# Two model blocks on one core: memory products placed between the features behind each norm, one modulation chunk's columns moved behind a gathering, and half of two norms' squares moved to VectorE

## The reference, cut to what matters

```python
for layer in range(DEPTH):                                  # first block
    mod = (c_act @ ada_w[layer] + ada_b[layer])[:, None, :]
    sh1, sc1, g1, sh2, sc2, g2 = jnp.split(mod, 6, axis=-1)
    h = rms_norm(x, norm1_g[layer]) * (1.0 + sc1) + sh1
    x = x + g1 * mixer(h)                                   # even or odd mixer
    h = rms_norm(x, norm2_g[layer]) * (1.0 + sc2) + sh2
    x = x + g2 * grouped_moe(h, ...)
for layer in range(DEPTH):                                  # second block
    x = x + rms_norm_2(mixer_2(rms_norm_2(x, g[0])), g[1])
    mem_n = rms_norm_2(mem, mem_norm_g[layer])
    k = mem_n @ wk[layer]; v = mem_n @ wv[layer]            # 256 x 256 each: the "memory products"
    q = rms_norm_2(x, g[2]) @ wq[layer]
    x = x + rms_norm_2(softmax_attention(q, k, v) @ wo[layer], g[3])
    x = x + rms_norm_2(swiglu(rms_norm_2(x, g[4]), ...), g[5])
```

## Time and profile before

| | before |
|---|---|
| median of 3 runs | 1759.46 us (1755.81 to 1762.49) |
| the profiled execution, its own time | 1757.93 us |
| its span in the trace | 1756.1 us |
| PE busy | 1672.5 us (95%) |
| DVE busy | 1272.7 us (72%) |
| ACT busy | 1091.1 us (62%) |
| HBM read | 411.21 MB, 235 GB/s over the span |
| mean granted PE clock | 0.983 of 2.4 GHz |

### The profile page before, as it was taken

How to read it: one execution, slowest core, us unless ns; L and a number is a source line. 1 busy time by engine, 2 the same in 40 slices (tenths; PEclk the granted TensorE clock), 3 DMA queues, 4 the chain that set the end, 5 groups by cost and what they waited for, 6 DMA issues and landing times.

```text
span 1756.1 us, 25101 instructions
## 1 busy us (share of the span) xinstructions
PE 1672.5 (95%) x8563; PEld 1355.7 (77%) x8563; DVE 1272.7 (72%) x2053; ACT 1091.1 (62%) x1681; POOL 13.1 (1%) x27
## 2 busy tenths in 40 slices
PE   5998999999999999999999898899999998999998
PEld 3875778888878767888888786678888776878886
DVE  3874598988977586989989656666666656676665
ACT  3545488888864464887988655665444547564443
POOL 1000000000000000000000000000000000000000
PEclk8999899999999998999999999999999999999999
DMA  9878489999977573999999654115565561325552
GB/s 367 301 266 330 183 323 331 383 330 348 370 260 262 192 222 114 354 325 376 340 334 384 233 168 144 49 72 193 182 200 187 163 215 49 136 91 183 191 191 72
DMA packets 113346, 413.37 MB, mean 235 GB/s; under 512 B 13024, under 2 KB 13072, under 8 KB 112880
## 3 DMA queue, kind: packets, MB, share of 16 engines
q1 hardware_dynamic: 110208, 400.74, 64.3%
q0 software_dynamic: 1936, 8.59, 1.5%
q10 hardware_dynamic: 1120, 2.99, 0.4%
HBM read 411.21 MB, written 1.05 MB: 235 GB/s over the span
## 4 chain that ended last, share of the span: by engine, by line
PE 78%; DVE 8%; ACT 7%; issue 3%; DMA 3%; DVEq 0%; ACTq 0%; SPq 0%
PE banks L794 17%; PE banks L796 16%; PE banks L795 16%; PE banks L1604 9%; PE banks L1605 5%; DVE weights_low L2309 2%; PE banks L966 2%; ACT weights_high L2016 1%; DMA weight_ring<-in_exp_w_gate 1%; PE banks L925 1%; PE banks L824 1%; DMA weight_ring<-in_ada_w 1%; ACT qk_features L1925 1%; PE banks L851 1%; ACT scratch L1863 1%
## 5 line engine op out<-in xcount | busy, mean ns | idle before, releaser
L2309 DVE TENSOR_TENSOR weights_low<-weight_ring,weights_high 128x1024 fp32r<-128x1024 f32 (+1 forms) x656 | 769.3, 1218 | 145.1 <-ACT weights_high L1691 84.7
L794 PE MATMUL banks<-weights_high,features_parts 128*128 128x512 f32 (+1 forms) x1488 | 591.8, 398 | 11.8 <-DVE features_parts L2573 3.6
L796 PE MATMUL banks<-weights_high,features_parts 128*128 128x512 f32 (+1 forms) x1488 | 580.9, 390 | 0.0
L795 PE MATMUL banks<-weights_low,features_parts 128*128 128x512 f32 (+1 forms) x1488 | 580.4, 390 | 0.0
L2016 ACT ACTIVATE weights_high<-weight_ring 128x1024 fp32r<-128x1024 f32 x384 | 392.9, 1061 | 80.6 <-PE banks L796 52.9
L794 PEld LDWEIGHTS banks<-weights_high,features_parts 128*128 128x128 f32 x1488 | 280.9, 189 | 78.6 <-issue 13.3
L796 PEld LDWEIGHTS banks<-weights_high,features_parts 128*128 128x128 f32 x1488 | 280.5, 189 | 59.9
L795 PEld LDWEIGHTS banks<-weights_low,features_parts 128*128 128x128 f32 x1488 | 281.1, 189 | 55.3 <-issue 0.7
L1691 ACT ACTIVATE weights_high<-weight_ring 128x1024 fp32r<-128x1024 f32 (+1 forms) x176 | 176.9, 1044 | 125.6 <-PE banks L796 45.0
L1604 PE MATMUL banks<-features_parts,weights_high 128*128 128x512 f32 x704 | 250.7, 400 | 1.1 <-DVE features_parts L2448 1.0
L1605 PE MATMUL banks<-features_parts,weights_low 128*128 128x256 f32 x704 | 197.7, 281 | 0.0
(11 more groups left out here) (413 smaller groups left out, 1626.1 us busy)
## 6 DMA issues: line engine op xcount, KB each, us to landing
weight_ring<-in_exp_w_gate SPq DMA_DIRECT2D x128, 512.0 KB, 5.2
weight_ring<-in_exp_w_up SPq DMA_DIRECT2D x128, 512.0 KB, 5.1
weight_ring<-in_exp_w_down SPq DMA_DIRECT2D x128, 512.0 KB, 5.3
weight_ring<-in_ada_w SPq DMA_DIRECT2D x84, 512.0 KB, 5.5
weight_ring<-in_ffn_wg SPq DMA_DIRECT2D x44, 512.0 KB, 4.1
weight_ring<-in_ffn_wu SPq DMA_DIRECT2D x44, 512.0 KB, 4.5
weight_ring<-in_ffn_wd SPq DMA_DIRECT2D x44, 512.0 KB, 4.1
weight_ring<-in_even_w_in SPq DMA_DIRECT2D x28, 512.0 KB, 5.7
```

What stands on the lines that cost most here:

```text
L794: eng.matmul(dst, lh, rh, start=first, stop=False, **kw)
L795: eng.matmul(dst, lh, rl, start=False, stop=False, **kw)
L796: mm = eng.matmul(dst, ll, rh, start=False, stop=last, **kw)
L2309: V(half_of(low(s), i, size), half_of(slot(n), i, size), half_of(high(s), i, size).bitcast(F32), ALU.subtract)\
```

## The change

It does five things, named as above.

(a) In `experts(0)` the four products of `modulate(15)` go behind `gather(0)`, and the two filling products go out.
(b) Behind the first experts PE makes 12 memory steps, and the last 4 stand one by one ahead of the turns 4 to 7, where the 8 filling products were.
(c) In the two norms ACT squares row block 0 alone, and DVE squares row block 1 with one `tensor_tensor_reduce`.
(d) In `cross(l)` PE makes 8 steps, waits until DVE has copied the last output chunk of the mixer (bank 5 or 7, where the second half of the product now goes), makes 2 steps, and puts the last 6 one by one ahead of the products k = 2 to 7. ACT copies the two halves with two instructions.
(e) In `feed_forward(0)` it makes 10 steps, and the last 6 likewise ahead of k = 2 to 7.

In the diff `norm_x(n)` and `take_mem_apart` are ACT's functions, `square_second_rows` is DVE's, and the others are PE's; ACT's `norm_whole_x` changes as `norm_x(n)` does.

```diff
-                    if i >= 4 and busy:
-                        stay_busy(4, busy[i - 4])
+                    ahead(i)
...
-            def by_feature(source, first=0):
+            def by_feature(source, first=0, between=lambda k: None):
                 def fresh(k):
                     if 1 <= k < 5:
                         turn_feature(source, k + 3, first=first)
+                    between(k)
                     features_wait()
...
-                if step == 2 * KD - 1:
-                    mm.then_inc(mem_used, 1)
+                    if step == 2 * KD - 1:
+                        mm.then_inc(mem_used, 1)
...
+                stay_busy(0, 0 if l == 0 else 4)
+                eng.wait_ge(rows_by_vector, 6 * l + 2)
+                gather(5 * l)
                 if l == 0:
                     modulate(15, 6, at=260)
-                stay_busy(0, 2 if l == 0 else 4)
-                eng.wait_ge(rows_by_vector, 6 * l + 2)
-                gather(5 * l)
...
-            mem_steps(16, [half_of(B[5], i, 512) for i in range(2)])
-            turn_normed("a1h1", (2, 2, 2, 2))
+            first_memory = [half_of(B[5], i, 512) for i in range(2)]
+            mem_steps(12, first_memory)
+            turn_normed("a1h1", lambda i: mem_steps(1, first_memory) if i >= 4 else None)
...
-                mem_steps(16, [B[2 + i][:, S:2 * S] for i in range(2)])
-                fresh = features_of_x(busy=0)
+                memory = [B[2][:, S:2 * S], B[5 + 2 * l][:, 0:S]]
+                mem_steps(8, memory)
+                eng.wait_ge(copied["dve"], chunks[st[("ev_out", "od_out")[l]][1][1][1]]["done"])
+                mem_steps(2, memory)
+                fresh = features_of_x(busy=0, between=lambda k: mem_steps(1, memory) if k >= 2 else None)
...
+                memory = [B[2 + i][:, S:2 * S] for i in range(2)]
                 if l == 0:
-                    mem_steps(16, [B[2 + i][:, S:2 * S] for i in range(2)])
-                fresh_x = features_of_x(4, 12 * l)
+                    mem_steps(10, memory)
+                fresh_x = features_of_x(4, 12 * l, lambda k: mem_steps(1, memory) if l == 0 and k >= 2 else None)
...
             def norm_x(n):
                 warm(ACT.Sqrt)
+                eng.wait_ge(x_ready, 2 * n - 1)
+                square(NB[:, 0, :], X[:, 0, :], 0)
+                eng.wait_ge(squares, sq[0])
...
+            def take_mem_apart(m, halves):
+
+                kind, l = MEM_ORDER[m]
+                eng.wait_ge(mem_used, m + 1)
+                for i in range(2):
+                    ins = eng.activation((MK if kind == "k" else MV)[l][:, i, :], halves[i], ACT.Copy)
+                ins.then_inc(mem_taken, 1)
...
+            def square_second_rows(at):          # DVE
+
+                eng.tensor_tensor_reduce(NB[:, 1, :], X[:, 1, :], X[:, 1, :], 1.0, 0.0, ALU.mult, ALU.add, SS[:, at:at + 1])\
+                   .then_inc(var_ready, 1)
```

More of the change, by code:

```diff
@@ L812, in stay_busy, with turn @@
                                start=True, stop=True, skip_group_check=True)
-            def turn(name, source, busy=()):
+            def turn(name, source, ahead=lambda i: None):
                 first, items = turns[name]
@@ L872, in by_pair, with features_of_x @@
                     features_wait()
-            def features_of_x(first=0, busy=12):
+            def features_of_x(first=0, busy=12, between=lambda k: None):
                 for tb in range(TB):
@@ L881, in features_of_x @@
                         turn_feature(of_x, k, [tb], first)
-                return by_feature(of_x, first)
+                return by_feature(of_x, first, between)
             def chunk(q, steps, fresh=None):
@@ L966, in mem_steps, with turn_normed @@
                     mm = eng.matmul(halves[i], left, right, start=k == 0, stop=k == KD - 1)
-                if step == 2 * KD - 1:
-                    mm.then_inc(mem_used, 1)
+                    if step == 2 * KD - 1:
+                        mm.then_inc(mem_used, 1)
             normed_n = [0]
-            def turn_normed(name, busy=()):
+            def turn_normed(name, ahead=lambda i: None):
                 normed_n[0] += 1
                 eng.wait_ge(normed, normed_n[0])
-                turn(name, lambda i, tb: NB[:, tb, i * 128:(i + 1) * 128], busy)
+                turn(name, lambda i, tb: NB[:, tb, i * 128:(i + 1) * 128], ahead)
             def attention(pairs, between=lambda t: None, first=lambda t: None):
@@ L1771, in norm_x @@
                 warm(ACT.Sqrt)
+                eng.wait_ge(x_ready, 2 * n - 1)
+                square(NB[:, 0, :], X[:, 0, :], 0)
+                eng.wait_ge(squares, sq[0])
                 for tb in range(TB):
-                    if n:
-                        eng.wait_ge(x_ready, 2 * n - 1 + tb)
-                    elif tb == 0:
-                        eng.wait_ge(x_loaded, 16)
-                    square(NB[:, tb, :], X[:, tb, :], tb)
-                    if n:
-                        eng.wait_ge(squares, sq[0])
-                        eng.activation(ROOT[:, tb:tb + 1], SS[:, tb:tb + 1], ACT.Sqrt, scale=1.0 / D, bias=EPS_[:, :])\
-                           .then_inc(root_ready, 1)
-                if not n:
-                    eng.wait_ge(squares, sq[0])
-                    take_root(SS, TB, D)
+                    if tb:
+                        roots[0] += 1
+                        eng.wait_ge(var_ready, roots[0])
+                    eng.activation(ROOT[:, tb:tb + 1], SS[:, tb:tb + 1], ACT.Sqrt, scale=1.0 / D, bias=EPS_[:, :])\
+                       .then_inc(root_ready, 1)
             def norm_and_take_raw(l):
@@ L1829, in norm_whole_x @@
                 warm(ACT.Sqrt)
+                eng.wait_ge(x_ready, done - 1)
+                square(NB[:, 0, :], X[:, 0, :], 4)
+                eng.wait_ge(squares, sq[0])
                 for tb in range(TB):
-                    eng.wait_ge(x_ready, done - 1 + tb)
-                    square(NB[:, tb, :], X[:, tb, :], 4 + tb)
-                    eng.wait_ge(squares, sq[0])
+                    if tb:
+                        roots[0] += 1
+                        eng.wait_ge(var_ready, roots[0])
                     eng.activation(ROOT[:, 2 + tb:3 + tb], SS[:, 4 + tb:5 + tb], ACT.Sqrt, scale=1.0 / D, bias=EPS_[:, :])\
@@ L2201, in cross @@
                 eng.wait_ge(features_split, features[0] + 8)
-                take_mem(1 + 2 * l, PS[:, 2:4, S:2 * S])
+                take_mem_apart(1 + 2 * l, (B[2][:, S:2 * S], B[5 + 2 * l][:, 0:S]))
                 take_chunks(st[f"caq{l}"][1], lambda i: QK[:, i, :])
@@ L2362, in normalise @@
                 ins.then_inc(normed, 1)
+            def square_second_rows(at):
+                eng.tensor_tensor_reduce(NB[:, 1, :], X[:, 1, :], X[:, 1, :], 1.0, 0.0, ALU.mult, ALU.add, SS[:, at:at + 1])\
+                   .then_inc(var_ready, 1)
             def norm_x():
-                sqn[0] += TB
+                sqn[0] += 1
+                square_second_rows(1)
                 for tb in range(TB):
@@ L2501, in norm_whole_x @@
             def norm_whole_x():
-                sqn[0] += TB
+                sqn[0] += 1
+                square_second_rows(5)
                 for tb in range(TB):
```

## The result

The changed kernel takes 1766.81 us (median of 6 runs, 1764.88 to 1770.99) where the kernel before takes 1760.07 us in its 6 (1753.67 to 1763.22). The ratio is 1.0046, with a 95% interval of 1.0028 to 1.0065: slower by nearly half a per cent. The ratio is formed over all runs; the two medians alone give 1.0038, which lies in the same interval. The profiled execution took 1764.88 us, with a span of 1763.1 us, 7.0 us longer than that of before. The mean granted clock is 0.982 (0.983 before).

A forecast was written before the change was run, and what follows sets the result against it. PE, busy 1672.5 of 1756.1 us, was taken as the bound, except where SP waits on a memory product. Terms 6.9 + 4.4 + 0 - 1.6 - 0.4 + 0.6 = +9.9 us; forecast 1768.5 us, range 1762 to 1775.

The forecast's parts named there:

- cross(0): Attention to the memory, layer 0: memory tile's release and gate tile 7.5 us later, up tile's split 6.9 later; +6.9 us.
- The rival that the load is hidden: Both crosses: later loads stay hidden, only PE's exchange is left; 1758.5 us, not slower; chance 0.1.
- no slack: cross(0) before the change: ACT waits for the gate tile, the scores stand behind ACT, and nothing is spare.
- cross(1): Attention to the memory, layer 1: SP issues 7.5 us later, ACT starts on the up tile later; +4.4 us.
- The feed-forward part: Layer 0: the next three tiles come 7 us later, covered by 13 us of gate and up products; 0.
- Behind the first experts: Norm there: moved steps replace eight filling products, real work removed, so transposes start 1.6 us sooner; -1.6 us.
- The whole norm: Behind the second experts: without ACT's second square the second diagonal comes sooner and PE's pause goes; -0.4 us.
- The gathering: In experts(0): starts 0.64 us sooner, but four modulation products then stand ahead of the transposes; +0.6 us.
- DVE's square at half rate: Both norms: the square takes 2.6 us instead of 1.3, +2.0 on the sum, 1770.5 us; rival, chance 0.15.
- The stalls cost less than the shift: Attention in the crosses: PE's clock changes phase, some half-clock work runs full, worth 0.5 to 2 us; 1767; chance 0.2.
- my own sum: Whole kernel: the terms of all changed places together, +9.9 us; chance 0.45.

The follow-up runs named there:

- experiment 5: Changed kernel with all 16 memory steps ahead of bare transposes behind the first experts, and experts(0)'s modulation behind the gathered rows' transposes: ratio 1.0054 to the kernel before.
- experiment 6: Changed kernel with both rows' squares of the two norms on ACT again: ratio 1.0034 to the kernel before.
- experiment 8: Kernel before plus both norm edits, gate tile split behind each attention to the memory, up tile split in feed_forward(l): 1752.49 us, ratio 0.9961.

## Why the prediction was right, point by point

The direction and the mechanism were right and the size nearly so: 1768.5 us forecast, 1766.8 measured. The closeness is in part luck. The sum was +9.9 us; the measured shift is +6.7 between the medians and +7.0 between the two traces, and of these 7.0 the changed places make 5.8, while 1.2 come from stretches that the change does not touch. The measurement lies 0.46% above before, just inside the 0.5% up to which I counted no change, for which I had 0.42; the 0.55 for slower by more than that was a little too much.

- **cross(0)**, forecast +6.9. The ledger has +6.6, SP issued the next memory tile 14.64 us behind the first memory step (1147.15 to 1161.79) where it was 7.32 before, and PE stood 7.05 us. The rival that the load is hidden fell with ACT's 8.88 us. One sentence of the prediction was wrong, that there was no slack. Before the change, behind both gate splits and the first copies, ACT waited for PE's last query product:

```profile
1165.24 0.38 ACT L1735 ACTIVATE qk_features<-banks 128x256 f32<-128x256 f32 x1 [0.69 <-PE banks L796]
```

  These 0.7 us are why a release 7.3 us later made the scores only 6.6 us later. The sum had them in it all the same, since it counted from the start of the up tile's split at 1165.52, which stands behind this wait. The four copies, taken as 1.2 us, took 0.95.
- **cross(1)**, forecast +4.4, measured +3.7. The first half landed 3.64 us behind its issue where I had worked out 3.9 from cross(0), SP issued 14.63 us behind the first memory step where I had 14.8, and ACT's four copies took 0.95 us instead of 1.2.
- **The feed-forward part**, forecast 0. The ledger has -0.6. About half of it is a wait that the moved steps filled, PE's for the last feature before the eighth product, which is gone in the changed kernel:

```profile
1199.12 0.19 PEld L1604 LDWEIGHTS banks<-features_parts,weights_high 128*128 128x128 f32 x1 [0.36 <-DVE features_parts L2448]
```

  The other 0.3 us are products that follow each other a little faster at the same granted clock (2.08 us instead of 2.12 for six pairs), and why is open.
- **Behind the first experts**, forecast -1.6, measured -1.8. My step that the moved memory steps take the place of removed filling work was half right: experiment 5 shows that the fillings were hidden, and that it is the steps' new place that gains, with 0.4 us of DVE's square on top (experiment 6).
- **The whole norm**, forecast -0.4, measured -0.5. DVE's square took 1.23 us and 0.08 for its sum, where I took 1.3.
- **The gathering**, forecast +0.6, measured +0.4, by the path that I had: the transposes start 0.33 us later after the router, and ACT and DVE both wait for them last. The gathering began 0.57 us sooner (0.64 forecast) and took 3.79 us instead of 3.96, and the four products held the transposes back by 1.07 us (their loads take 1.24, between the 1.83 and the 0.9 that I had for the two clock levels). What I did not see is that DVE needs these columns too; experiment 5 shows it, where the transposes stand first.
- **DVE's square at half rate** (0.15) fell: 1.23 us for 1024 columns is 1.2 ns a column, less than the 1.64 of the form with one operand in PSUM, not twice that. The forms of 128 and 256 columns take 287 and 420 ns in the trace before, 1.04 ns for each further column; from 256 to the 1024 columns of the new square it is 1.05. The Trainium skill, Vector Engine (DVE) Microarchitecture Reference, section Points that are easy to get wrong, has a rule of half throughput for `S2S2D2_STT` with two non-bf16 sources in SBUF. The trace names this instruction `CUSTOM_DVE_ANT_0`, so no run here shows whether the rule is meant for it; it did not run at half rate with both operands in SBUF as fp32.
- **The stalls cost less than the shift** (0.2, 0.5 to 2 us) came true beside my own sum, with 2.0 us, and it is the largest piece of the 4.1 us by which the changed places fell short of my +9.9. Before, the clock was 0.57 of full in the stretch where PE turns weights and multiplies values; after, it is low in the scores, which take 2.99 us instead of 1.60, and full behind them. Before, then after:

```profile
1174.00:1178.00 4.00, 3.70 (x20) 2.71 (x22) 2.06 (x5) 0.68 (x2) 0.00 (x0) 0.57 0.00 0
```

```profile
1171.70:1175.70 4.00, 3.86 (x18) 2.96 (x19) 3.19 (x6) 3.46 (x5) 0.00 (x0) 0.62 0.02 4
...
1180.60:1182.40 1.80, 1.76 (x16) 1.27 (x16) 1.63 (x4) 0.60 (x1) 0.00 (x0) 1.00 0.00 0
```

Behind the scores PE waits for DVE in any case, and so slow scores cost little: that wait shrinks from 2.54 to 1.14 us while the turned weights and values behind it gain 1.3 us. That a PE at work without such long waits keeps its clock fits experiment 8, where the same stretch runs at full clock all through; what makes the clock fall was not tested by itself.

What stays open: what makes the clock fall in a stretch of one trace and not of another, where the kernels are the same up to there. The +1.2 us of the ledger outside the changed stages are of that kind and are not shown to be the change's.

## What to carry to other kernels

Before moving the last read of a buffer later, follow its release through the whole queue: the next load, every load behind that one, and every engine that waits in order for one of these ahead of work that somebody else needs; here six steps of 0.43 us, put where each looked free, delayed a release by 7.3 us, and SP, the DMAs and ACT passed 6.6 of it on to PE. An engine that splits or copies for a later stage should do so behind the copies that the present stage waits for, and as late as the consumer allows, which here was worth more than the change that was tried. Work that is put into an idle gap gains only what it takes away from a place where the engine is the pacer, and moving a product out of one engine's way can make its result the last thing that another engine waits for, as the modulation products did in experiment 5 (0.13 us gained of 1.1).

## What the runs showed of the hardware

- A fused square and sum on DVE (`tensor_tensor_reduce`, 128 x 1024 fp32, both operands the same tile in SBUF) takes 1.23 us and 0.08 us for reading its sum, against 1.06 and 0.19 us on ACT beside it.
- The same instruction took 287 ns at 128 columns, 420 at 256 (one operand in PSUM) and 1226 at 1024 (both in SBUF).
- Two halves of a 1 MB tile, issued 0.85 us behind another tile in one queue, let ACT start 6.5 to 6.8 us after the first tile's issue in three runs; as the first in the queue they let it start after 3.64 us.
- After an idle time of 7.05 us PE went on at 0.62 of full clock in its next 4 us, and was at 1.00 behind that; where the longest idle time there was 0.85 us (experiment 8), it stayed at 1.00.
